# Block-wise modulation of the first norm, written as columns on the transposed rows

## The reference

```python
mod = jax.nn.silu(c) @ w_ada[l] + b_ada[l]
shift1, scale1, gate1, shift2, scale2, gate2 = [m[:, None, :] for m in jnp.split(mod, N_MOD, axis=-1)]
h = rmsnorm(x, norm1_g[l]) * (1.0 + scale1) + shift1
proj = h @ w_in[l]
(q_a, k_a, v_a, q_b, k_b, v_b, q_i, k_i, w_i, g_a, g_b) = jnp.split(proj, IN_OFFSETS, axis=-1)
```

## Time and profile before

| | |
|---|---|
| median of 3 runs | 897.79 us (896.08 to 898.65) |
| the profiled execution | 893.21 us, span 891.4 us |
| PE busy | 803.2 us, 90% of the span |
| DVE, ACT, POOL busy | 614.2, 432.1, 73.3 us |
| DMA | 174.94 MB, mean 196 GB/s |

### The profile page before, as it was taken

One profiled execution on the slowest core, in us unless ns is written; L12 is line 12 of the kernel. 1 busy time (PEld: TensorE's weight loads), 2 busy tenths in 40 slices (PEclk: granted clock), 3 DMA queues, 4 the chain that ended last, 5 costly groups with the idle time before them and its releaser, 6 DMA issues.

```text
span 891.4 us, 10532 instructions
## 1 busy us (share of the span) xinstructions
PE 803.2 (90%) x3988; PEld 640.1 (72%) x3988; DVE 614.2 (69%) x739; ACT 432.1 (48%) x504; POOL 73.3 (8%) x67
## 2 busy tenths in 40 slices
PE   1239999999999979999999759999999999999993
PEld 0028878787666646667888758888888888888882
DVE  3685895122699986553654863979788888888882
ACT  1323214245655545556221634656657575756660
POOL 4020000000000000000000000011111121111111
PEclk9959999999999999999999758999999999999998
DMA  9918958020111131132273251989898989989873
GB/s 317 332 55 323 344 192 314 0 77 19 48 41 56 47 95 48 48 133 81 95 261 142 92 201 60 326 266 347 313 343 309 348 293 328 313 310 336 308 240 51
DMA packets 74809, 174.94 MB, mean 196 GB/s; under 512 B 7272, under 2 KB 16584, under 8 KB 71696
## 3 DMA queue, kind: packets, MB, share of 16 engines
q1 hardware_dynamic: 69712, 156.81, 48.7%
q0 software_dynamic: 5056, 17.59, 8.0%
HBM read 163.86 MB, written 10.52 MB: 196 GB/s over the span
## 4 chain that ended last, share of the span: by engine, by line
PE 83%; DVE 7%; DMA 4%; ACT 2%; issue 1%; POOL 1%; SPq 0%; POOLq 0%; DVEq 0%; ACTq 0%
PE ps L581 21%; PE ps L583 20%; PE ps L582 20%; PE ps L902 7%; PE ps L699 4%; DMA raw<-in_w_ada 2%; DVE acc L1378 1%; PE ps L681 1%; PE ps L783 1%; PE ps L799 1%; PE ps L811 1%; DMA acc<-in_b_ada 1%; PE ps L714 1%; PE ps L727 1%; PE ps L951 1%
## 5 line engine op out<-in xcount | busy, mean ns | idle before, releaser
L1646 DVE TENSOR_TENSOR w_lo<-raw,w_hi 128x2048 fp32r<-128x2048 f32 x96 | 216.9, 2286 | 23.1 <-ACT w_hi L1284 22.5
L1284 ACT ACTIVATE w_hi<-raw 128x2048 fp32r<-128x2048 f32 x96 | 181.8, 1913 | 15.9 <-PE ps L583 15.9
L1368 DVE TENSOR_TENSOR w_lo<-raw,w_hi 128x2048 fp32r<-128x2048 f32 (+1 forms) x28 | 62.1, 2218 | 71.7 <-ACT w_hi L1018 71.4
L581 PE MATMUL ps<-act_lo,w_hi 128*128 128x512 f32 x232 | 98.3, 424 | 8.8 <-DVE w_lo L1368 7.8
L581 PE MATMUL ps<-w_lo,hgT_hi 128*128 128x512 f32 x256 | 101.0, 395 | 0.0
L582 PE MATMUL ps<-w_hi,hgT_lo 128*128 128x512 f32 x256 | 99.8, 390 | 0.0
L583 PE MATMUL ps<-w_hi,hgT_hi 128*128 128x512 f32 x256 | 99.7, 389 | 0.0
L583 PE MATMUL ps<-act_hi,w_hi 128*128 128x512 f32 x232 | 91.6, 395 | 0.0
L582 PE MATMUL ps<-act_hi,w_lo 128*128 128x512 f32 x232 | 91.3, 394 | 0.0
L1018 ACT ACTIVATE w_hi<-raw 128x2048 fp32r<-128x2048 f32 (+1 forms) x28 | 51.8, 1855 | 80.3 <-DMA raw<-in_w_in 43.9
L560 POOL DMA_INDIRECT out<-ys,slot_tok x16 | 49.0, 3061 | 320.3 <-DVE ys L1742 246.2
(11 more groups left out here) (244 smaller groups left out, 1448.6 us busy)
## 6 DMA issues: line engine op xcount, KB each, us to landing
raw<-in_w_gate SPq DMA_DIRECT2D x32, 1024.0 KB, 8.5
raw<-in_w_up SPq DMA_DIRECT2D x32, 1024.0 KB, 6.4
raw<-in_w_down SPq DMA_DIRECT2D x32, 1024.0 KB, 8.7
raw<-in_w_ada SPq DMA_DIRECT2D x24, 1024.0 KB, 7.1
raw<-in_w_in SPq DMA_DIRECT2D x18, 1024.0 KB, 6.4
...
```

The costliest lines, as they stand in the source:

```text
L581: pe.matmul(o, a[0], b[1], start=start, stop=False)
L1284: act.activation(e_hi[s_][:, :], e_raw[r][:, :], ACT.Copy).then_inc(e_top, 1)
L1368: dve.tensor_tensor(lo, r, hi.bitcast(F32), ALU.subtract).then_inc(chunk_split, 1)
L1646: dve.tensor_tensor(e_lo[s_][:, :], e_raw[r][:, :], e_hi[s_][:, :].bitcast(F32), ALU.subtract).then_inc(e_split, 1)
```

## The change

The modulation of the first norm is made in five blocks of channels, `PARTS` = (0), (1), (2, 3), (4, 5), (6, 7), each channel block 128 wide, and as columns (one value per partition) instead of rows. x is scaled by 1/rms alone, transposed by PE, and the gain and shift are applied to the transposed blocks (`hfull`). The chunks of ada0 are replaced by `ad0` (the columns of scale and shift of one block, all rows; eight chunks) and misc and qb by `mq` (the rows of one block, all columns of misc and qb; five chunks). For blocks 0 and 1 PE multiplies w_ada itself by the column silu(c) (`mod1_direct`, 16 matmuls of one column); for the others DVE does it in 512-wide steps (`mod1_step`) and PE sums (`mod1_sums`, 4 matmuls of one column) in the middle of the block before. PE accumulates misc and qb block by block (`mq_part`). x comes first, in four transfers. Two more raw buffers serve the 13 early chunks. POOL's memsets and loads for ada1 and ada2 no longer wait. The bias copies move from ACT to DVE, and the norm of q and k of branch B moves behind all chunks up to the second of qi, its square root on ACT behind `mod_rows(2)`.

```diff
-    raw = [at(f"raw{i}", [CH], F32, 8 * i) for i in range(RAW)]
+    raw = [at(f"raw{i}", [CH], F32, 8 * i) for i in range(RAW)] + [at(f"raw_early{i}", [CH], F32, 152 + 8 * i) for i in range(2)]
...
+                    for part in (1, 2) for k in range(KD)]
...
+        PARTS = [(0,), (1,), (2, 3), (4, 5), (6, 7)]
...
+        def add_mq(ks):
+            nk = len(ks)
+            rows = w_in[0][P * ks[0]:P * ks[0] + P * nk].rearrange("(k p) n -> p k n", p=P)
+            add_w("mq", [(0, 2 * DH, rows[:, :, C_KVB:C_KVB + 2 * DH]),
...
+                         (KVW + 2 * DH, MQW, rows[:, :, C_QB:C_QB + HW])], nk)
...
+        def add_mod(ks):
+            n, a = P * len(ks), P * ks[0]
+            step = KD // len(ks)
+            for c0 in range(0, KD, step):
+                rows = w_ada[0][P * c0:P * c0 + P * step].rearrange("(k p) n -> p k n", p=P)
+                add_w("ad0", [(0, n, rows[:, :, D + a:D + a + n]), (n, 2 * n, rows[:, :, a:a + n])], step)
+        add_mq(PARTS[0])
+        add_mod(PARTS[0])
+        add_mod(PARTS[1])
+        add_mq(PARTS[1])
+        for ks in PARTS[2:]:
+            add_mod(ks)
+            add_mq(ks)
+        N_EARLY = len(chunks)
...
-        mixed, rest = chunks[:KD], ada_list[KD:]
-        for ch, n in zip(chunks[KD:], (1, 2, 2, 2, 2, 2, 2, 2, 1, 0, 0, 0)):
-            mixed += [ch] + rest[:n]
+        mixed, rest = chunks[:N_EARLY], ada_list
+        for ch, n in zip(chunks[N_EARLY:], (0, 0, 4, 4, 3, 5, 0, 0)):
+            mixed += rest[:n] + [ch]
             rest = rest[n:]
         chunks = mixed
...
-        raw_slot = [n % RAW if n < N_PROJ else (n - N_PROJ) % 2 for n in range(N_RAW)]
+        raw_slot = [n % (RAW + 2) if n < N_EARLY else (n - N_EARLY) % RAW if n < N_PROJ else (n - N_PROJ) % 2
+                    for n in range(N_RAW)]
...
-        SEGS = [("ada0", 0, None), ("misc", 1, None), ("qb", 0, False), ("qa", 1, True), ("ada1", 0, None),
+        SEGS = [("misc", 1, None), ("qb", 0, False), ("qa", 1, True), ("ada1", 0, None),
...
-            elif n == first[name][-1] or name == "misc":
-                used.append((seg_ready, seg_done(name, 3)))
+            elif n == first[name][-1]:
+                used.append((seg_ready, seg_done("qb" if name == "mq" else name, 3)))
...
-            for n in range(3):
-                load(n)
-            sp.dma_start(xres[:, :, :], x[0].rearrange("(t p) d -> p t d", p=P)).then_inc(ld_x, 16)
-            sp.dma_start(g1row[:, :], norm1_g.partition_broadcast(P).rearrange("p a d -> p (a d)")).then_inc(ld_rows, 16)
-            for n in range(3, N_RAW):
+            xv = x[0].rearrange("(t p) d -> p t d", p=P)
+            for tt in range(NT):
+                sp.dma_start(xres[:, tt], xv[:, tt]).then_inc(ld_x[tt], 16)
+            for n in range(N_RAW):
                 load(n)
...
-            link(pool.memset(acc[0][:, :], 0.0))
...
+            pool.dma_start(bgrow[0:2 * KD, :], b_ada[0, 0:2 * D].rearrange("(r p) -> r p", p=P)).then_inc(ld_bg, 16)
+            pool.dma_start(bgrow[2 * KD:3 * KD, :], norm1_g[0].rearrange("(r p) -> r p", p=P)).then_inc(ld_bg, 16)
...
-                if part == 1:
-                    pool.wait_ge(hT_ps, 2 * NT)
-                pool.wait_ge(seg_ready, seg_done("ada0", 3))
...
-            ada_seg(0)
...
             for tt in range(NT):
                 pe.wait_ge(h_rows, tt + 1)
-                for g in range(2):
-                    n = 2 * tt + g
...
+                for k in range(KD - 1):
+                    last = x_turned(tt, k, k)
+            last.then_inc(xT_ps, 1)
...
+            def mod1_direct(u):
...
+                pe.wait_ge(raw_in[raw_slot[n]], fill[n])
+                for j in range(2):
+                    for k in range(KD):
+                        a = 2 * P * k + P * j
+                        last = pe.matmul(mod1_at(u, j, j + 1), raw[raw_slot[n]][:, a:a + P], sc_col[:, k:k + 1],
+                                         start=(k == 0), stop=(k == KD - 1))
+                last.then_inc(mod1_ps, 1)
+            def mod1_sums(u):
+                split_ready(first["ad0"][2 * u - 1])
+                for j in range(4):
+                    last = pe.matmul(mod1_at(u, j, j + 1), accm[u % 2][:, P * j:P * j + P], ones[:, 0:1],
+                                     start=True, stop=True)
+                last.then_inc(mod1_ps, 1)
...
+            def mq_part(u):
+                ks = PARTS[u]
...
+                split_ready(n)
...
+                for i, kk in enumerate(ks):
+                    pe.wait_ge(hT_sp, kk + 1)
...
+                    last = three(b0[:, :], wp(i, KVW, KVW + 2 * DH), tuple(x_[:, kk, :] for x_ in H), kk == 0, kk == KD - 1)
...
+                for tt in range(NT):
...
+                        wh, wl = wp(i, 0, KVW)
...
+                        last = pe.matmul(o, xh, wh, start=False, stop=(kk == KD - 1), skip_group_check=True)
...
+                for m in range(4):
+                    if m == 3 and u == 0:
+                        pe.wait_ge(mod1_sb, 2)
+                    if m == 2 and 2 <= u + 1 < len(PARTS):
+                        mod1_sums(u + 1)
+                    for i, kk in enumerate(ks):
+                        last = three(bank("qb", m)[:, :], tuple(x_[:, kk, P * m:P * m + P] for x_ in H),
+                                     wp(i, KVW + 2 * DH, MQW), kk == 0, kk == KD - 1)
+                    if final:
+                        last.then_inc(seg_ready, 1)
+                if not final:
+                    last.then_inc(w_used, 1)
...
+            pe.wait_ge(sc_ready, 1)
+            mod1_direct(0)
+            pe.wait_ge(xT_dve, 1)
             for tt in range(NT):
-                last = misc_group(bank("misc", 1 + tt // 2)[:, KVW * (tt % 2):KVW * (tt % 2) + KVW], 0, KVW, tt)
-                if tt % 2:
-                    last.then_inc(seg_ready, 1 + tt // 2)
-            seg("qb", H)
+                last = x_turned(tt, KD - 1, KD - 2)
+            last.then_inc(xT_ps, 1)
+            pe.wait_ge(xT_act, 3)
+            mod1_direct(1)
+            pe.wait_ge(const_ready, 1)
+            for u in range(len(PARTS)):
+                mq_part(u)
+            pe.wait_ge(mod1_sb, len(PARTS))
             seg("qa", H)
             ada_seg(1)
...
-            for _ in range(2):
...
+            def h_high(u):
+                ks = PARTS[u]
+                act.wait_ge(mod1_sb, u + 1)
...
+                    act.activation(hfull[:, k % 4, :], xT[:, k, :], ACT.Identity, bias=mod1[:, 0, k:k + 1],
+                                   scale=mod1[:, 1, k:k + 1]).then_inc(h_act, 1)
+                act.wait_ge(h_dve, u + 1)
+                act.activation(act_hi[:, ks[0], :], hfull[:, ks[0] % 4, :], ACT.Copy).then_inc(hT_hi, 1)
...
+                    act.wait_ge(h_act, u - 1)
+                    act.activation(act_hi[:, ks[1], :], hfull[:, ks[1] % 4, :], ACT.Copy).then_inc(hT_hi, 1)
...
+            high(next(todo))
+            for k in (1, 2, 3):
+                x_copy(k, k, 1)
+            h_high(0)
+            x_copy(KD - 1, KD - 2, 2)
+            high(next(todo))
+            h_high(1)
+            for u in range(2, len(PARTS)):
                 high(next(todo))
-            for m in range(2):
...
+                h_high(u)
+            high(next(todo))
             high(next(todo))
...
             high(next(todo))
-            act.wait_ge(qk_var, 1)
-            act.activation(st[:, :, :], st[:, :, :], ACT.Sqrt, bias=epsc[:, 0:1], scale=1.0 / DH).then_inc(qk_sd, 1)
+            act.wait_ge(st_bias, 16)
             high(next(todo))
-            act.wait_ge(st_bias, 16)
...
             mod_rows(2)
             high(next(todo))
+            act.wait_ge(qk_var, 1)
+            act.activation(st[:, :, :], st[:, :, :], ACT.Sqrt, bias=epsc[:, 0:1], scale=1.0 / DH).then_inc(qk_sd, 1)
             seg_copy("qi", qiT)
             high(next(todo))
             act.preload_act_table_set("natural_log_exp_and_others")
...
+            dve.wait_ge(bias_ps, 2)
...
             for tt in range(NT):
...
+                dve.wait_ge(h_sd, tt + 1)
+                link(dve.reciprocal(st[:, tt, 1:2], st[:, tt, 1:2]))
+                dve.tensor_scalar(xres[:, tt, :], xres[:, tt, :], st[:, tt, 1:2], None, ALU.mult).then_inc(h_rows, 1)
+            raw_chunks(1)
...
-            raw_chunks(first["ka"][0] + 1 - KD - 1)
+            def mod1_step(u):
+                for c_ in range(2):
+                    n = next(todo)
+                    dve.wait_ge(raw_in[raw_slot[n]], fill[n])
+                    for q in range(4):
+                        w_ = raw[raw_slot[n]][:, 512 * q:512 * q + 512]
+                        k = 4 * c_ + q
+                        if k == 0:
+                            link(dve.tensor_scalar(accm[u % 2][:, :], w_, sc_col[:, 0:1], None, ALU.mult))
+                        else:
+                            last = dve.scalar_tensor_tensor(out=accm[u % 2][:, :], in0=w_, scalar=sc_col[:, k:k + 1],
```

(21 more changed lines are left out.)

208 lines of the change are left out of this document (108 added, 100 removed).

## The result

The changed kernel takes 883.5 us (median of 4 runs, 882.05 to 887.0), the kernel before 897.1 us (median of 4, 896.08 to 898.65). The ratio is 0.985, 95% interval 0.982 to 0.989: 13.6 us less, by the interval 10 to 16. The forecast was 884.1 us. Run again later in five rounds, the same kernel gave 884.3 us.

A forecast was written before the change was run, and what follows sets the result against it. PE's time and gaps bound the kernel up to 202.10 us; six terms sum to -13.7 us, giving 879.5 from the profiled 893.21, plus 4.6 to the median: 884.1 us. Own range 880 to 888, with A and C 875 to 893.

The forecast's parts named there:

- the six terms: Opening -32.5, blocks +4.2, qa to qi +1.0, va's first chunk +1.8, step behind va +9.8, clock behind that gap +2.0 us.
- The opening: Before the first projection: projections begin at 33.7 instead of 66.2 us, -32.5 us.
- first tile is ready at 12.7 us: In the opening: DVE's row scaling waits for its bias copies, done at 11.8 us, and delivers x's first tile at 12.7.
- unknown costs: Effects no row prices; among them POOL's memsets beside DVE's row scaling in the opening, 0 to +3.6 us.
- rival A: Clock is high in the opening: direct products 4.1 us each, projections begin near 25 us, kernel 875 us; 20%.
- a sign of being wrong: In the opening: direct products running at the high clock, instead of about 6.9 us each, would show the prediction wrong.
- the two paces that the prediction weighed: Direct products in the opening: 214 ns a pass at clock 0.50, which it took, or the skill's 107 ns.
- The blocks: Projections of misc and qb by blocks: 44.2 us for 40.0, +4.2 us, with 4 us at half the clock.
- ada1 and va: PE waits for ada1's last chunk after qa, +1.0 us, and for va's first chunk after qi, +1.8 us.
- rivals C and D: C (15%): 1 MB load stream lags, 887 to 893 us; D (5%): column pieces load slowly, kernel ends at 907.
- The step behind va: ACT's split of g0 waits for va's end, other ACT work queues behind: gates start 10.6 us after va, +9.8 us.
- The clock behind the gap: Behind the idle gap after va, PE runs 4.0 us at clock 0.50: +2.0 us, bounds 0 and 4.

The follow-up runs named there:

- experiment 4: Changed kernel, but POOL starts its two accumulator memsets only when DVE has scaled the last tile of x: 880.9 us.
- experiment 12: Changed kernel timed and profiled once more with nothing edited: 884.3 us.
- experiment 8: Changed kernel with qa's first chunk in raw buffer 1 and DVE's split of va's first chunk ahead of the norm of q and k: 879.2 us.
- Experiments 1, 2 and 3: Changed kernel, split buffers two further on: 871.7 us; kernel before, split buffers one further on: 906.5 us; changed kernel, ACT's g0 split behind va's copies: 880.3 us.
- before_clash: Kernel before, split buffers numbered one further on so va's second chunk and the first gate chunk share buffer 0: 906.5 us, ratio 1.011.

## Why the prediction was right

The time lies 0.6 us from the forecast, and the terms have the right signs and places. But the agreement is closer than the working deserves: by PE's lead the six terms measured -33.0, +7.4, +1.2, +1.6, +9.5 and +1.6, together -11.7 us where the prediction has -13.7. (The lead is 33.0 us at the first projection, 25.7 at qa, 24.5 behind ada1's sums, 22.9 in va, 13.3 at the gates and 11.7 from 192.8 us on.) In detail:

**The opening: -33.0 for -32.5, by two errors that cancel.** The step "first tile is ready at 12.7 us" failed: it was ready at 14.8 and the last at 19.1, because POOL's memsets stopped DVE (experiment 4). It was listed among the unknown costs with 0 to +3.6 us and taken at 0, since "transposes are slower than the scaling anyway"; it is 3.5 us. Against it, the first direct product took 3.85 us, not 6.9: rival A's price, for one of the two products. The second took 6.83. The prediction had named direct products at the high clock as a sign of being wrong, and for one of the two the sign came. That the two errors cancel is luck. Of the two paces that the prediction weighed for these passes, both occur: 0.12 us a pass in the first product, 0.21 in the second, and by experiment 12 the first product can have either. The Trainium skill's rule (TensorE: Matmul & The Clock Gate, LDWEIGHTS) is 107 ns for 128 columns and names no clock. It is near the fast pace; by it the slow one should not be there, and it is, in 11 of the 18 products of the nine profiles in which they are whole and unchanged.

**The blocks: +7.4 for +4.2.** From 33.20 to 80.58 us are 47.4 us, 40.0 before. The sums and the wait of 1.2 us for DVE came as counted. What was mis-sized is the first stretch at half the clock: taken as 4 us, as in the kernel before, it was 9.0 us (33.2 to 42.2), which costs 2.5 us more. Some 0.7 us are left that I did not trace.

**ada1 and va: waits of 0.9 us for 1.0, and 1.3 for 1.8.** Both stand in the list at their places, and experiment 8 takes them away. PE's lead falls by 1.2 and 1.6 us there. The working for ada1 gives 101.2 less 99.7, 1.5 us, and not the 1.0 that was counted. PE waits for no load between 40 and 140 us, so of rivals C and D nothing more is seen than this.

**The step behind va: 9.5 for 9.8.** The gates begin 10.1 us behind va's end (178.66 to 188.76), 10.6 forecast, and began 0.7 us behind it before (201.45 to 202.10), 0.8 by the prediction. Experiments 1, 2 and 3 show the mechanism from three sides. This was read from the order of instructions, not from any wait in the trace of before.

**The clock behind the gap: about 1.6 for 2.0.** PE's lead over before is 13.3 us at 188.76, and 11.7 us at the last bias product of branch A's steps (L785, at 300.5 us; L701 at 312.2 before).

**The two spans differ by 8.6 us alone, not by 13.7.** From a lead of 11.7 us at 300 us, 1.9 are lost between 321 and 326 us (granted clock 0.67 in the window of 316 to 324 us, where the profile of before has 1.00), 0.5 won back near 530 us, and 1.7 lost behind the last transposes of the experts. The work there is the same in both kernels. `before_clash`, whose work behind the gates is that of the kernel before, has such a stretch too (0.91 in the window of 340 to 360 us), so such losses come without the change too. The execution profiled before was 3.9 us under its median (the kernel before spreads from 893.2 to 899.2 us in this study), the one after 1.1 us over. So the medians lie 13.6 us apart where PE's lead is 11.7: about 2 us of the agreement come from which executions were profiled and not from the mechanism, and that the forecast met the median within 0.6 us is in part luck. Adding the profile's distance to the median was the better choice all the same; comparing the two spans would have shown less than two thirds of the gain.

The gain was thus 33 us of opening, of which 20 were given back by the time the gates begin, 9.5 of them through a buffer number that costs 12 us in all, the slow clock behind it included.
